# First stage of a two-block float32 kernel: who splits the gate weights, who modulates, and who sums the first modulation

## The reference

```python
mod = silu_c @ ada_w + ada_b                     # c is one vector of 1024, ada_w 1024 x 3072
shift, scale, gate = jnp.split(mod, 3, axis=-1)
h = rms_norm(x, norm_pre_w) * (1.0 + scale) + shift
z = h @ w_in                                     # 1024 x 6144; one part of it is f_pre, the forget gate
...                                              # pooling, a gated recurrence, output product, block two
```

## Time and profile before

| what | value |
|---|---|
| median of 3 executions | 1230.07 us (1227.62 to 1231.0) |
| profiled execution, first to last instruction | 1229.2 us |
| TensorE, VectorE, ScalarE, GpSimd busy, share of the span | 96%, 60%, 39%, 10% |
| instructions | 14679 |
| bytes from and to memory, mean rate | 116.69 MB, 95 GB/s |

### The profile page before, as it was taken

One profiled execution on the slowest core, in us unless ns is written; L12 is line 12 of the kernel. 1 busy time (PEld: TensorE's weight loads), 2 busy tenths in 40 slices (PEclk: granted clock), 3 DMA queues, 4 the chain that ended last, 5 costly groups with the idle time before them and its releaser, 6 DMA issues. The chain is left out here.

```text
span 1229.2 us, 14679 instructions
## 1 busy us (share of the span) xinstructions
PE 1178.8 (96%) x5722; PEld 967.7 (79%) x5724; DVE 732.5 (60%) x1183; ACT 477.4 (39%) x775; POOL 124.7 (10%) x111
## 2 busy tenths in 40 slices
PE   4999998899999999989999999999999999999997
PEld 3778877787888877877788878887778888888886
DVE  6786579777658832464677989345644343343433
ACT  4146333414347733255335334333553222222223
POOL 3210234552300110010000000000000000000000
PEclk8899998988999999999999999999999999999999
DMA  6553322232211152223222222222112222222211
GB/s 234 197 187 103 112 94 70 70 101 69 71 68 52 52 191 84 97 86 117 72 86 70 86 73 99 83 87 71 52 56 99 103 87 102 103 86 103 96 59 69
DMA packets 32533, 116.69 MB, mean 95 GB/s; under 512 B 3776, under 2 KB 3776, under 8 KB 32464
## 3 DMA queue, kind: packets, MB, share of 16 engines
q1 hardware_dynamic: 30672, 109.88, 26.5%
q0 software_dynamic: 1648, 5.83, 1.4%
q10 hardware_dynamic: 144, 0.03, 0.0%
HBM read 113.64 MB, written 2.10 MB: 94 GB/s over the span
## 5 line engine op out<-in xcount | busy, mean ns | idle before, releaser
L967 DVE TENSOR_TENSOR w_lo<-raw,w_hi 128x1024 fp32r<-128x1024 f32 (+2 forms) x173 | 216.5, 1254 | 273.9 <-ACT w_hi L552 272.4
L1533 PE MATMUL acc<-hT_hi,w_hi 128*128 128x512 f32 x904 | 366.8, 406 | 4.6 <-issue 2.9
L1535 PE MATMUL acc<-hT_hi,w_lo 128*128 128x512 f32 x904 | 356.4, 394 | 0.0
L1534 PE MATMUL acc<-hT_lo,w_hi 128*128 128x512 f32 x904 | 356.4, 394 | 0.0
L552 ACT ACTIVATE w_hi<-raw 128x1024 fp32r<-128x1024 f32 (+3 forms) x181 | 187.1, 1036 | 130.2 <-PE acc L1535 127.3
L1533 PEld LDWEIGHTS acc<-hT_hi,w_hi 128*128 128x128 f32 x904 | 173.2, 192 | 44.8 <-issue 9.1
L1535 PEld LDWEIGHTS acc<-hT_hi,w_lo 128*128 128x128 f32 x904 | 172.3, 191 | 37.3
L1534 PEld LDWEIGHTS acc<-hT_lo,w_hi 128*128 128x128 f32 x904 | 173.2, 192 | 35.7 <-issue 1.4
L1533 PE MATMUL acc<-w_hi,hT_hi 128*128 128x512 f32 (+1 forms) x160 | 63.6, 397 | 0.2
L1586 PEld LDWEIGHTS side<-xq 128*128 128x128 f32 x384 | 49.6, 204 | 16.5 <-DVE xq L983 15.2
L1535 PE MATMUL acc<-w_hi,hT_lo 128*128 128x512 f32 (+1 forms) x160 | 61.8, 386 | 0.0
(11 more groups left out here) (358 smaller groups left out, 1792.2 us busy)
## 6 DMA issues: line engine op xcount, KB each, us to landing
raw<-in_ga SPq DMA_DIRECT2D x32, 512.0 KB, 3.2
raw<-in_ada SPq DMA_DIRECT2D x16, 512.0 KB, 4.4
raw<-in_wo SPq DMA_DIRECT2D x16, 512.0 KB, 3.5
raw<-in_br SPq DMA_DIRECT2D x16, 512.0 KB, 3.2
raw<-in_q SPq DMA_DIRECT2D x8, 512.0 KB, 4.1
raw<-in_u SPq DMA_DIRECT2D x8, 512.0 KB, 3.4
raw<-in_gp SPq DMA_DIRECT2D x8, 512.0 KB, 3.9
raw<-in_ada_w SPq DMA_DIRECT2D x8, 512.0 KB, 3.6
```

Of the source, the lines that this page charges most:

```text
L967: nc.vector.tensor_tensor(out=w_lo[:, k % SPLITS, 0:width], in0=raw[:, n % RING, 0:width], in1=w_hi[:, k % SPLITS, 0:width].bitcast(f32), ...
L1533: nc.tensor.matmul(ps, w[0], x[0], start=first, stop=False)
L1534: nc.tensor.matmul(ps, w[0], x[1], start=False, stop=False)
L1535: return nc.tensor.matmul(ps, w[1], x[0], start=False, stop=last)
```

## The change

Three things change in the first stage, and nothing behind it.

1. GpSimd's loop over the eight `("fk", k)` units (L469) is gone. VectorE makes these `w_lo` in its own order, by `split_lo(k + 1)` between `lower_h(k + 1)` and part 1 of the next sums.
2. VectorE's multiply-and-shift of the tile (L948) is gone. ScalarE does it twice from the plain transposed x, with scale and shift as operands for each partition: once rounded into `hT_hi`, once in full into `hT_full` (`modulate_h`). For tile 0 it reads the transposed x from PSUM. The copies out of PSUM are put in another order, for which the transposes are issued in the order `XT_ORDER`.
3. For tile 0 alone, VectorE multiplies and adds only strips 0 to 3. Strips 4 to 7 go straight to TensorE, as eight float32 matmuls with silu(c) as the moving column (`BY_PE`).

```diff
+BY_PE = [strip for strip in range(4, 8)]
+XT_ORDER = [7, 0, 1, 3, 4, 2, 5, 6]
+XT_COPIES = [7, 1, 2]
+def ada_count(kind, j):
+    return 16 + j if kind == "gate_ada" else max(j, 1)
...
@@ SyncE
-                    if last[0] in ADA:
-                        sp.wait_ge(ada_summed, last[1] + 1 + 16 * (last[0] == "gate_ada"))
+                    if last == ("ada", 1):
+                        sp.wait_ge(mod_summed, 1)
+                    elif last[0] in ADA:
+                        sp.wait_ge(ada_summed, ada_count(*last))
...
@@ GpSimd
-            for k in range(KT):
-                n = UNIT["fk", k]
-                pool.wait_ge(hi_made, k + 1)
-                nc.gpsimd.tensor_tensor(out=w_lo[:, k % SPLITS, 0:7 * P], in0=raw[:, n % RING, 0:7 * P],
-                                        in1=w_hi[:, k % SPLITS, 0:7 * P].bitcast(f32), op=ALU.subtract)\
-                    .then_inc(lo_made, 1)
...
@@ ScalarE
+            def modulate_h(kt):
+                act.wait_ge(scale_made, kt + 1)
+                if kt in range(3, 7):
+                    act.wait_ge(xT_taken, kt - 2)
+                elif kt:
+                    act.wait_ge(xT_copied, XT_COPIES.index(kt) + 1)
+                else:
+                    act.wait_ge(xT_made, XT_ORDER.index(0) + 1)
+                src = hT_full[:, kt, :] if kt else acc[0][:, :]
+                scale, shift = scale_a[:, kt:kt + 1], mod[:, kt:kt + 1]
+                nc.scalar.activation(hT_hi[:, kt, :], src, ACT.Identity, scale=scale, bias=shift).then_inc(h_hi, 1)
+                nc.scalar.activation(hT_full[:, kt, :], src, ACT.Identity, scale=scale, bias=shift).then_inc(h_full, 1)
+            copy_xT(7)
             split_hi(0)
-            for kt in (7, 0, 1, 2):
-                act.wait_ge(xT_made, kt + 1)
-                nc.scalar.activation(hT_full[:, kt, :], (acc + side)[kt][:, :], ACT.Copy).then_inc(xT_copied, 1)
...
-            upper_h(0)
+            copy_xT(1)
+            modulate_h(0)
+            copy_xT(2)
...
                 if k + 1 < KT:
-                    upper_h(k + 1)
+                    modulate_h(k + 1)
...
@@ VectorE, sum_modulation
+                    if kt == 0 and strip in BY_PE:
+                        continue
...
@@ VectorE, modulate
-                nc.vector.tensor_scalar(hT_full[:, kt, :], hT_full[:, kt, :], scale_a[:, kt:kt + 1], shift,
-                                        ALU.mult, ALU.add).then_inc(h_full, 1)
...
@@ TensorE, sum_mod
+                direct = BY_PE if kt == 0 else []
...
+                    for strip in direct:
+                        at_ = (strip % 4) * 256 + o * P
+                        nc.tensor.matmul(ps, raw[:, n % RING, at_:at_ + P], silu_c[:, strip:strip + 1],
+                                         start=(strip == direct[0]), stop=False)
```

More of the change, by code:

```diff
@@ L941, in modulate @@
                                              op=ALU.add))
[L942 to L947, removed]
-                nc.vector.tensor_scalar(hT_full[:, kt, :], hT_full[:, kt, :], scale_a[:, kt:kt + 1], shift,
-                                        ALU.mult, ALU.add).then_inc(h_full, 1)
+                nc.vector.scalar_tensor_tensor(out=scale_a[:, kt:kt + 1], in0=scale, scalar=1.0,
+                                               in1=par[:, PAR["pre_w"]][:, kt:kt + 1], op0=ALU.add, op1=ALU.mult)\
+                    .then_inc(scale_made, 1)
             def lower_h(kt):
@@ L964, in split_lo @@
                 for u in ORDER[before + 1:n]:
-                    add_ada(*u)
+                    if u[0] == "gate_ada":
+                        add_ada(*u)
                 dve.wait_ge(hi_made, k + 1)
@@ L1207, in _ @@
             then(nc.vector.reciprocal(tmp8, tmp8))
-            then(nc.vector.tensor_tensor(out=silu_c, in0=tmp8, in1=par[:, PAR["c"]], op=ALU.mult))
+            nc.vector.tensor_tensor(out=silu_c, in0=tmp8, in1=par[:, PAR["c"]], op=ALU.mult).then_inc(silu_made, 1)
+            dve.wait_ge(silu_made, 1)
             for t in range(TT):
@@ L1213, in _, with take_xT @@
             sum_modulation(0, 0)
-            sum_modulation(0, 1)
-            for kt in range(3, 7):
-                dve.wait_ge(xT_made, kt + 1)
+            def take_xT(kt):
+                dve.wait_ge(xT_made, XT_ORDER.index(kt) + 1)
                 nc.vector.tensor_copy(hT_full[:, kt, :], (acc + side)[kt][:, :]).then_inc(xT_taken, 1)
-                if kt == 4:
-                    modulate(0)
+            take_xT(3)
+            take_xT(4)
+            modulate(0)
+            split_lo(0)
+            take_xT(5)
             lower_h(0)
+            take_xT(6)
             sum_modulation(1, 0)
@@ L1232, in _ @@
                     lower_h(k + 1)
+                    split_lo(k + 1)
                     if k + 2 < KT:
@@ L1743, in _ @@
                 pe.wait_ge(x_normed, t + 1)
-                for kt in range(KT):
+                for kt in XT_ORDER:
                     ins = nc.tensor.transpose((acc + side)[kt][:, t * P:(t + 1) * P], x_in[:, t, kt * P:(kt + 1) * P],
@@ L1750, in sum_mod @@
             def sum_mod(kt):
-                pe.wait_ge(ada_summed, 2 * kt + 2)
+                direct = BY_PE if kt == 0 else []
+                n = UNIT["ada", 2 * kt + 1]
+                if direct:
+                    pe.wait_ge(raw_in[n % RING], 16 * (n // RING + 1))
+                    pe.wait_ge(silu_made, 1)
                 if kt:
-                    pe.wait_ge(h_full, kt)
+                    pe.wait_ge(scale_made, kt)
                 for o in range(2):
+                    ps = side[3][:, 8 * o + kt:8 * o + kt + 1]
+                    for strip in direct:
+                        at_ = (strip % 4) * 256 + o * P
+                        nc.tensor.matmul(ps, raw[:, n % RING, at_:at_ + P], silu_c[:, strip:strip + 1],
+                                         start=(strip == direct[0]), stop=False)
+                    pe.wait_ge(ada_summed, ada_count("ada", 2 * kt + (not direct)))
                     for a in range(2):
-                        ins = nc.tensor.matmul(side[3][:, 8 * o + kt:8 * o + kt + 1],
-                                               ada_acc[:, kt % 2, a, o * P:(o + 1) * P], ones[:, 0:1],
-                                               start=(a == 0), stop=(a == 1))
+                        ins = nc.tensor.matmul(ps, ada_acc[:, kt % 2, a, o * P:(o + 1) * P], ones[:, 0:1],
+                                               start=(a == 0 and not direct), stop=(a == 1))
                 ins.then_inc(mod_summed, 1)
-            pe.wait_ge(xT_copied, 1)
+            pe.wait_ge(xT_copied, 1 + XT_COPIES.index(7))
             sum_mod(0)
@@ L1774, in _ @@
                         if j == 0:
-                            pe.wait_ge(xT_copied, h + 2) if h < 3 else pe.wait_ge(xT_taken, h - 2)
+                            if h in XT_COPIES:
+                                pe.wait_ge(xT_copied, XT_COPIES.index(h) + 1)
+                            elif h:
+                                pe.wait_ge(xT_taken, h - 2)
                         ins = product((acc + side)[h][:, :], (hi[:, cols], lo[:, cols]), (hT_hi[:, j, :], hT_lo[:, j, :]),
```

15 lines of the change are left out of this document (7 added, 8 removed).

## The result

| | before | changed |
|---|---|---|
| median of 9 executions, us | 1228.36 (1225.33 to 1234.21) | 1222.69 (1219.06 to 1224.62) |
| ratio to before, 95% interval | 1 | 0.9942 [0.9926, 0.9959] |
| profiled execution, span in us | 1229.2 | 1221.0 |
| first small operation of tile 0 and of tile 1 | 17.86, 25.51 | 16.92, 25.06 |
| six periods from there, together | 46.65 | 40.40 |

The kernel is faster by 0.58%, 7.1 us (5.0 to 9.1), clear of the 0.3% that can be told from no change. That is the ratio of all executions on either side; the two medians lie 5.7 us apart. Before had three runs when the forecast was made, and its median was 1230.07; nine give 1228.36.

A forecast was written before the change was run, and what follows sets the result against it. VectorE's chain plus a return through TensorE was taken to bound each period of the first stage. 1.1 us at the start and 4.4 in six periods made 5.5, from 1230.07 to 1224.6 us, range 1222.0 to 1227.4.

The forecast's parts named there:

- Rival 3: First stage: the stretched addition is not GpSimd's doing; periods of 8.6 us, end at 1234; chance 0.02.
- The steps of a period: First stage: start and end times within one steady period of the changed kernel, summing to 6.71 us against 7.51.
- the term for the six periods: First stage, periods between 25.51 and 72.16 us: 4.4 us saved, with part of the low clock kept.
- high-clock bound: Six periods of the stage at the high clock throughout: 6 x 6.71 = 40.3 us, a saving of 6.4.
- The bound of 2.7: Six periods with the granted clocks of before, TensorE's work taken as 5.7 us: together 43.9, a saving of 2.7.
- The start: Start of the stage: with twelve float32 matmuls for tile 0, the strips of tile 1 come 1.1 us sooner.
- Rival 5: Start of the stage: direct matmuls cost twice the measured 0.255 us; gain 3.4, time 1226.7; chance 0.02.
- the trace disagrees: Float32 matmuls on TensorE: the skill says four passes; four matmuls left eight records, two for each.
- The end of the stage and what follows: Last split, for `("f", 7)`: VectorE stays ahead by half a microsecond, so nothing is paid; what follows is unchanged.

The follow-up runs named there:

- e5: The kernel before with part 1 alone: VectorE instead of GpSimd makes the lower parts of the gate weights; median 1219.91 us, ratio to before 0.9924.
- e3: The changed kernel with part 1 undone: GpSimd makes the lower parts of the gate weights again; median 1226.38 us, ratio to before 0.9977.
- e7: The changed kernel with eight GpSimd subtractions of 896 columns added, on tiles nobody else uses then; one run, 1230.32 us.
- e8: The changed kernel with eight GpSimd fills of 896 columns added, which only write; one run, 1224.64 us.
- e11: The kernel before once more, with nothing added, for a second trace; one run, 1225.36 us.
- e1: The changed kernel once more, no edit; median 1221.24 us, ratio to before 0.9938.
- e9: The kernel before with six unused matmuls added ahead of each sum from tile 2 on, filling TensorE's idle time; median 1227.18 us, ratio 0.9987.
- e2: The changed kernel with part 3 undone: VectorE adds all eight strips of tile 0; median 1223.02 us, ratio to before 0.9948.
- e6: The changed kernel with the next weights rounded ahead of the modulation and split ahead of `lower_h`; median 1215.86 us, ratio to before 0.9892.

## What the prediction had right, and the step that failed

**The bound and the mechanism were right.** VectorE's chain set the period: "a period is VectorE's chain ... plus a return through TensorE". The addition that stood still was GpSimd's doing: it goes with GpSimd's split (changed, e5), comes back with it (e3), and comes back with a GpSimd operation that reads tiles of its own (e7). Rival 3 falls with this. The Trainium skill, in "SBUF — State Buffer", section "Who interferes with whom", has the same rule: VectorE and GpSimd share a pair of ports as an exclusive lock, and a VectorE instruction with two SBUF inputs contends with a GpSimd instruction that reads SBUF, not with one that only writes it. For reading, 2345 against 472 ns agree; for writing, e8 agrees as far as it goes, with a fill of 0.85 us under the split and 0.84 without it.

**The steps of a period** were right within 0.06 us:

| step, from the first small operation | predicted | measured (period at 45.25) |
|---|---|---|
| end of ScalarE's pair | 2.02 | 1.97 |
| start of `lower_h` | 2.03 | 2.01 |
| start of the split | 2.90 | 2.85 |
| start of the last four strips | 3.90 | 3.87 |
| TensorE's sums | 5.62 | 5.68 |
| period | 6.71 | 6.74 |

An activation with two operands for each partition took 0.80 to 0.82 us; 0.81 was taken.

**The step that failed is the term for the six periods,** in which the forecast weighed the low clock. It took 4.4 us, between 2.7 with the clocks of before and 6.4 with the high clock throughout. The pair of first traces gives 6.25, and 40.40 is the 40.3 of the high-clock bound. With the second traces (45.20 in e11, 40.98 in e1) the four pairings give 4.2 to 6.3, 5.2 in the mean. Two things were wrong in that step.

- The bound of 2.7 charged the first period with 5.7 / 0.71 = 8.03. That period has less work: 21 matmul records where the others have 30, since the first products of tile 0 run before it. It lasted 6.73 at a clock of 0.60, and 6.73 in e1 at 0.70. With 6.71 in its place the bound is 4.0, and the middle between it and 6.4 is 5.2. Where all 30 records stand the working held: 5.7 / 0.77 is 7.40, and the period at 0.77 in e1, with TensorE busy throughout, lasted 7.31.
- The forecast kept a part of the low stretches that the first trace of before showed in its later periods. The first trace of the changed kernel has no such period and e1 has one. Nor were they a fixed property of the kernel before, whose second trace loses 1.45 us less to them.

Why the clock falls in one trace and not in another stays open. The forecast had argued that less idle time of TensorE brings more of the high clock; e9 and e11 do not settle it.

**The start** was taken as 1.1 us to the second tile, at 24.4. It came at 25.06 and 23.98, against 25.51 and 25.70 before: 0.45 for the first pair, 1.72 for e1 against e11, 1.1 in the mean of the four pairings. The size is right, its reason was not: the forecast let part 3 bring the gain, while e2 and e5 have it without part 3. It had seen that the six additions of tile 0 run beside a split of GpSimd's, but did not ask what part 1 alone does to them: one of them took 2.30 us and takes 0.48, and TensorE's sums begin at 14.97 in e5 instead of 16.80. Rival 5 falls: the eight direct matmuls took 1.05 and 1.03 us, four each, the 0.26 a matmul that was priced. That each leaves two records tells this price; how many passes through the array lie in a record, no trace here shows, so the forecast's "the trace disagrees" says more than they do.

**The end of the stage and what follows** went as said: 11.77 us from the last modulation to the head (11.75 before), and no new wait behind it.

**In all,** the head starts 5.4 to 7.2 us sooner, 6.3 in the mean, over the four pairings of two traces each, and the totals say 7.1 (5.0 to 9.1); 5.5 was forecast, at the low end of both. The 0.8 between 6.3 and 7.1 is less than the spread of what follows the stage. The forecast also treated the three parts as a whole whose sum counts. It saw that the split costs 1.0 on the path and that the pair brings waits, but did not add up part 2 by itself: 0.47 saved against 0.27 and 0.27 of new waits, so nothing. That sum, from the same rows, would have told before any run that part 1 is the whole change. Nor did it ask whether the two waits could be ordered away, which is worth 3.9 to 4.4 us more at the head (e6).

## What to carry to other kernels

Look in the trace for one long instruction among short ones of the same form, and for what runs beside it: work moved to an idle GpSimd can cost VectorE more than doing it itself, here 1.87 us for a split of 1.0. When work leaves a bounding engine for another, write down when the result comes back; if the first engine waits for it in the same round, nothing is gained until the order lets it do something else meanwhile. Where a change has several parts, price each by itself, and compare stages by a mark in the trace, not by the total, when the total's spread is as large as the effect.

## What the runs showed of the hardware

- A GpSimd operation with SBUF inputs that runs for 2.2 to 2.5 us holds back the VectorE operation that begins under it until it ends: one addition of 0.47 us took 2295 to 2351 ns (before, e3, e9, e11), or 1901 to 1904 when it met it later (e7), and a conversion with one input 1702 instead of 220. It does so on tiles that have nothing to do with each other. The other way round, the same GpSimd subtraction took 1.68 us alone and 2.52 when it began under VectorE's split (e7).
- A fill of 0.85 us that begins under VectorE's split is not held back and holds nothing back (e8). Whether a long fill holds back an addition that begins under it is not shown.
- The same instructions behind the stage took 1141.0 to 1146.2 us. Over the nine runs of the changed kernel the mean granted clock goes with the time: 0.988 at a span of 1217.3 us, 0.982 at 1222.9, and the seven others in order between them. So most of the 0.3% that limits the measurement goes with the clock.
